# The last layer's experts: each block's down product moved into its own turn

## The reference, cut to what matters

```python
def hier_moe(h, gw, gb, ew, eb, w_gu, w_down):
    ...
    w_sel = jax.nn.softmax(top_v, axis=-1) * p_g
    e_idx = g_sel[:, None] * EXPERTS_PER_GROUP + top_i
    combine = jnp.sum(jax.nn.one_hot(e_idx, N_EXPERTS, dtype=jnp.float32) * w_sel[..., None], axis=1)
    y = jnp.zeros((tok.shape[0], D), jnp.float32)
    for e in range(N_EXPERTS):
        gu = tok @ w_gu[e]
        act = jax.nn.silu(gu[:, :D_EXPERT]) * gu[:, D_EXPERT:]
        y = y + combine[:, e:e + 1] * (act @ w_down[e]).astype(jnp.float32)
    return y.reshape(B, L, D).astype(h.dtype)
```

## Time and profile before

| | |
|---|---|
| time, median of 3 runs | 1123.66 us (1121.16 to 1126.11) |
| profiled execution: its own time | 1126.82 us |
| profiled execution: span | 1125.1 us |
| mean granted TensorE clock over the span | 0.929 |
| from the start of the last layer's first gate_up to the end of its last add_rows | 885.5 to 1114.1 us |
| the same stretch, busy (885 to 1114.2 us) | PE 188.48 us, DVE 56.14 us, ACT 17.03 us, DMA share 0.90 |
| from the last add_rows to the end of the span | 11.0 us |

### The profile page before, as it was taken

The page is one execution under the profiler, slowest core; times in us unless marked ns, Lnnn a source line. Parts: engine busy times, 40 slices in busy tenths (PEclk is TensorE's granted clock), DMA queues, the critical chain, the costliest instruction groups (busy, mean ns, idle before and its releaser), DMA issues.

```text
span 1125.1 us, 24489 instructions
## 1 busy us (share of the span) xinstructions
PE 950.4 (84%) x9652; PEld 595.8 (53%) x9653; DVE 390.4 (35%) x1003; ACT 280.6 (25%) x756; POOL 185.1 (16%) x284
## 2 busy tenths in 40 slices
PE   3999999899999599998996379997998688798785
PEld 2453634555555467666763166664665455455443
DVE  2100026658543512111111184627653622222123
ACT  4122135356433111111110162134644100000001
POOL 0030012310012233433332321014001100000001
PEclk9999999999999599999998679998999698999888
DMA  9983315466233879999999797541314989999991
GB/s 376 366 266 119 150 75 208 183 222 250 75 117 127 347 302 404 422 424 423 423 425 425 255 399 280 225 147 78 114 75 160 383 329 426 425 425 400 429 409 57
DMA packets 54663, 313.53 MB, mean 279 GB/s; under 512 B 12203, under 2 KB 17445, under 8 KB 36021
## 3 DMA queue, kind: packets, MB, share of 16 engines
q1 hardware_dynamic: 33664, 279.19, 61.1%
q0 software_dynamic: 10192, 27.88, 7.0%
q10 hardware_dynamic: 10724, 5.29, 1.6%
HBM read 303.88 MB, written 14.75 MB: 283 GB/s over the span
## 4 chain that ended last, share of the span: by engine, by line
PE 71%; DMA 10%; DVE 7%; issue 5%; ACT 4%; ACTq 2%; POOL 0%; SPq 0%; DVEq 0%; POOLq 0%
PE psum L1005 10%; PE psum L556 8%; PE psum L919 8%; PE psum L786 6%; PE psum L1018 5%; PE psum L584 4%; PE psum L932 3%; DMA R<-in_exp_w_gu_dram 3%; DMA weights<-in_exp_w_gu_dram 3%; PE psum L513 3%; PE psum L680 2%; DMA spare_w<-in_exp_w_down_dram 2%; PE psum L943 2%; PE psum L548 2%; PE psum L795 2%
## 5 line engine op out<-in xcount | busy, mean ns | idle before, releaser
L556 PE MATMUL psum<-hT,weights 128*128 128x512 f32 (+1 forms) x336 | 120.0, 516 | 1.5 <-DVE hT L2110 1.5
L1005 PE MATMUL psum<-weights,lat 128*32 128x256 f32 x1568 | 95.5, 395 | 21.9 <-DMA weights<-in_exp_w_gu_dram 9.7
L919 PE MATMUL psum<-weights,lat 128*32 128x256 f32 x992 | 70.8, 442 | 27.0 <-issue 18.5
L556 PEld LDWEIGHTS psum<-hT,weights 128*128 128x128 f32 x336 | 64.4, 193 | 53.8 <-issue 47.5
L1005 PEld LDWEIGHTS psum<-weights,lat 128*32 128x32 f32 x1568 | 61.4, 114 | 52.3 <-issue 29.6
L1667 DVE TENSOR_REDUCE st<-psum 128x1 f32<-128x512 f32 (+1 forms) x96 | 56.7, 599 | 48.3 <-PE psum L670 20.8
L1824 DVE STREAM_TRANSPOSE lat<-lat 128x256 f32<-128x256 f32 x41 | 18.3, 445 | 151.6 <-PE psum L1005 146.0
L919 PEld LDWEIGHTS psum<-weights,lat 128*32 128x32 f32 x992 | 38.9, 125 | 57.0 <-issue 44.1
L1287 ACT ACTIVATE R<-psum,st 128x512 f32<-128x512 f32 (+1 forms) x78 | 48.0, 616 | 80.1 <-DVE st L1667 48.0
L786 PE MATMUL psum<-weights,hT 128*128 128x512 f32 x144 | 64.9, 606 | 0.0
L1974 DVE TENSOR_TENSOR lat<-lat,psum 128x128 f32<-128x128 f32 x23 | 9.0, 391 | 123.5 <-ACT lat L1431 122.9
(11 more groups left out here) (342 smaller groups left out, 1577.6 us busy)
## 6 DMA issues: line engine op xcount, KB each, us to landing
weights<-in_exp_w_gu_dram SPq DMA_DIRECT2D x42, 2048.0 KB
weights<-in_ada_w_dram SPq DMA_DIRECT2D x24, 2048.0 KB, 8.4
weights<-in_exp_w_down_dram SPq DMA_DIRECT2D x22, 2048.0 KB
hT<-in_exp_w_gu_dram SPq DMA_DIRECT2D x10, 2048.0 KB
R<-in_exp_w_gu_dram SPq DMA_DIRECT2D x10, 2048.0 KB
spare_w<-in_exp_w_down_dram SPq DMA_DIRECT2D x10, 2048.0 KB
weights<-in_w_in_dram SPq DMA_DIRECT2D x6, 2048.0 KB, 15.2
weights<-in_w_out_dram SPq DMA_DIRECT2D x4, 2048.0 KB, 10.1
```

Source lines behind the costliest of these rows:

```text
L556: mm = nc.tensor.matmul(t[:, lo:hi], w[:, k, col:col + P], hT[:, k, lo:hi], start=(k == 0), stop=(k == KD - 1))
L919: mm = nc.tensor.matmul(gu_ps[BLK * j:BLK * j + BLK, 0:256], xgT[:, k, :], w[:, k % 4, j, :, :], start=(k == 0), stop=(k == KD - 1), skip_ ...
L1005: mm = nc.tensor.matmul(gu_ps[BLK * j:BLK * j + BLK, 0:256], xgT[:, k, :], w[:, k % 4, j, :, :], start=(k == 0), stop=(k == KD - 1), skip_ ...
```

## The change

Each block's down product stands in the block's own turn. A turn becomes gate_up(g), select(g + 1), add_rows(g) (which now adds the rows of block g - 1), a wait for the dn piece, down(g). Block 0's turn stands ahead of the loops, with its down product behind the table products. `expert` has one loop body for all of its blocks in place of two. Both tables go into one PSUM bank, and one copy reads them. On ScalarE y_out(g) comes ahead of silu(g); on VectorE rows_turn comes behind the turn of the activations. After the loops only one add_rows is left. The diff:

```diff
             def slot_tables():
-                for job, key, places_ in ((("st", L), ("slot_hot", L), place_token), (("wt", L), ("place_weight", L), place_weight)):
-                    pe.wait_ge(*at(*key))
-                    t = take(*job, banks=(B_TABLE,))
+                t = take("st", L, banks=(B_TABLE,))
+                for which, (key, places_) in enumerate((("slot_hot", place_token), ("place_weight", place_weight))):
+                    pe.wait_ge(*at(key, L))
...
-                def down(done, place):
-                    pe.wait_ge(y_copied, done)
-                    pe.sem_inc(sem("pe_hold"), 1)
-                    pe.wait_ge(actT_ready, done)
+                def down(g, place):
+                    pe.wait_ge(actT_ready, g + 1)
...
-                def block(g, place, place_before, landed=None, in_extra=False):
+                def block(g, place, landed, in_extra=False):
                     gate_up(g, place, landed, in_extra)
                     select(g + 1)
-                    down(g, place_before)
                     add_rows(g)
+                    pe.wait_ge(sem(f"w_dn{place}"), landed[1])
+                    pe.sem_inc(sem("pe_hold"), 1)
+                    down(g, place)
+
+                def expert(triple, place, first=False):
...
+                    if first:
+                        with pe.If(n_blocks > 1):
+                            with pe.Fori(start + 1, start + n_blocks) as g:
+                                block(g, place, both)
+                    else:
+                        with pe.Fori(start, start + n_blocks) as g:
+                            block(g, place, both, in_extra)
...
+                pe.wait_ge(sem("w_dn0"), landed0)
+                down(0, 0)
...
-                    if not first:
-                        block(start, place, (place + 2) % 3, ((L + 1) * 16 if in_extra else landed_lo(L, triple, place), landed), in_extra)
-                    pe.wait_ge(sem(f"w_dn{place}"), landed)
-                    pe.sem_inc(sem("pe_hold"), 1)
-                    with pe.If(n_blocks > 1):
-                        with pe.Fori(start + 1, start + n_blocks) as g:
-                            block(g, place, place, in_extra=in_extra)
...
-                down(total, 0)
                 add_rows(total)
-                add_rows(total + 1)
...
-                act.sem_inc(y_copied, 1)
+                act.sem_inc(sem("rows_added"), 1)
...
                 with act.Fori(1, total) as g:
+                    y_out(g)
                     silu(g)
-                    y_out(g)
...
-                    v.sem_inc(sem("hot_weighted"), 1)
...
-                def weigh_rows(n):
-                    v.wait_ge(sem("rows_added"), n)
+                def weigh_rows(g):
+                    if not isinstance(g, int):
+                        v.wait_ge(sem("rows_added"), g + 1)
...
-                    rows_turn(g + 2)
...
                     nc.vector.transpose(actT[:, :, :].rearrange("p b s -> p (b s)"), act_rows).then_inc(actT_ready, 1)
                     v.wait_ge(actT_ready, g + 1)
+                    rows_turn(g + 2)
                     hot_rows(g + 2)
...
-                v.wait_ge(*at("read", "wt", L))
                 block(0)
+                tables = read(v, "st", L)[:, 0:2 * 64].rearrange("p (w b) -> p b w", w=2)[:, 0:COLS, :]
+                nc.vector.tensor_copy(slot_table[:, :, :], tables).then_inc(*mark("v_route1", ("read", "st", L)))
...
+                weigh_rows(0)
                 with v.Fori(1, total) as g:
                     block(g)
                     weigh_rows(g)
-                weigh_rows(total)
```

More of the change, by code:

```diff
@@ L892, in slot_tables @@
                 L, S = 1, "pe_route1"
-                for job, key, places_ in ((("st", L), ("slot_hot", L), place_token), (("wt", L), ("place_weight", L), place_weight)):
-                    pe.wait_ge(*at(*key))
-                    t = take(*job, banks=(B_TABLE,))
+                t = take("st", L, banks=(B_TABLE,))
+                for which, (key, places_) in enumerate((("slot_hot", place_token), ("place_weight", place_weight))):
+                    pe.wait_ge(*at(key, L))
                     for i in range(4):
                         for a in range(QUADS):
-                            mm = nc.tensor.matmul(t[BLK * a:BLK * a + BLK, 0:COLS], places_[:, i, :], block_last[:, i, :],
+                            mm = nc.tensor.matmul(t[BLK * a:BLK * a + BLK, which * 64:which * 64 + COLS], places_[:, i, :], block_last[:, i, :],
                                                   start=(i == 0), stop=(i == 3), skip_group_check=True)
-                    mm.then_inc(*mark(S, ("filled", *job)))
+                mm.then_inc(*mark(S, ("filled", "st", L)))
             def experts_last():
@@ L945, in add_rows @@
                     mm.then_inc(sem("rows_added"), 1)
-                def block(g, place, place_before, landed=None, in_extra=False):
+                def block(g, place, landed, in_extra=False):
                     gate_up(g, place, landed, in_extra)
                     select(g + 1)
-                    down(g, place_before)
                     add_rows(g)
-                gate_up(0, 0, (landed_lo(L, 0, 0), (uses(0) + 1) * 16))
+                    pe.wait_ge(sem(f"w_dn{place}"), landed[1])
+                    pe.sem_inc(sem("pe_hold"), 1)
+                    down(g, place)
+                def expert(triple, place, first=False):
+                    n_blocks = pe.value_load(tabs[L][0:1, ds(triple * 3 + (T_NB + place), 1)], min_val=1, max_val=MORE + 1)
+                    start = pe.value_load(tabs[L][0:1, ds(triple * 3 + (T_START + place), 1)], min_val=0 if first else 1, max_val=MAXBLK)
+                    landed = (triple + (uses(place) + 1)) * 16
+                    in_extra = isinstance(triple, int) and (triple, place) == (1, 0)
+                    both = ((L + 1) * 16 if in_extra else landed_lo(L, triple, place), landed)
+                    if first:
[5 more added lines that the diff above has]
+                            block(g, place, both, in_extra)
+                landed0 = (uses(0) + 1) * 16
+                gate_up(0, 0, (landed_lo(L, 0, 0), landed0))
                 select(1)
@@ L1939, in route @@
                              rs[:, 9:11, 0:nt].unsqueeze(3).to_broadcast([P, 2, nt, BLK]), ALU.mult), ("place_weight", L))
-                    for which, job in enumerate(("st", "wt")):
-                        nc.vector.tensor_copy(slot_table[:, :, which], read(v, job, L)[:, 0:COLS]).then_inc(*mark(S, ("read", job, L)))
             def rows_turn(count):
@@ L1960, in experts_last @@
                 act_ready, actT_ready, y_done = sem(f"act_ready{L}"), sem(f"actT_ready{L}"), sem(f"y_done{L}")
-                def weigh_rows(n):
-                    v.wait_ge(sem("rows_added"), n)
-                    v.sem_inc(sem("v_hold"), 1)
-                    nc.vector.tensor_copy(slot_now.unsqueeze(1), slot_table[:, ds(n - 1, 1), :]).then_inc(sem("slot_now"), 1)
-                    v.wait_ge(sem("slot_now"), n)
+                def weigh_rows(g):
+                    if not isinstance(g, int):
+                        v.wait_ge(sem("rows_added"), g + 1)
+                        v.sem_inc(sem("v_hold"), 1)
+                    nc.vector.tensor_copy(slot_now.unsqueeze(1), slot_table[:, ds(g, 1), :]).then_inc(sem("slot_now"), 1)
+                    v.wait_ge(sem("slot_now"), g + 1)
                     ts(hot_weight, C("tokens"), slot_now[:, 0:1], slot_now[:, 1:2], ALU.is_equal, ALU.mult).then_inc(sem("hot_weighted"), 1)
@@ L1981, in block @@
                     v.wait_ge(actT_ready, g + 1)
+                    rows_turn(g + 2)
                     hot_rows(g + 2)
                 total = v.value_load(tabs[L][0:1, T_TOTAL:T_TOTAL + 1], min_val=N_EXP, max_val=MAXBLK)
-                v.wait_ge(*at("read", "wt", L))
                 block(0)
+                tables = read(v, "st", L)[:, 0:2 * 64].rearrange("p (w b) -> p b w", w=2)[:, 0:COLS, :]
+                nc.vector.tensor_copy(slot_table[:, :, :], tables).then_inc(*mark("v_route1", ("read", "st", L)))
+                v.wait_ge(*at("read", "st", L))
+                v.wait_ge(*at("banks_zero"))
+                weigh_rows(0)
                 with v.Fori(1, total) as g:
```

## The result

The changed kernel takes 1116.08 us (median of 7 runs, 1111.10 to 1119.89), the kernel before 1123.66 in the same comparison: ratio 0.9921, interval 0.9899 to 0.9944. The forecast was 1112.9 us, ratio 0.9904, with a range of 1109.5 to 1116.5. The first median lies near the upper end of that range, nearer to rival A's 1116.7 than to the forecast, so it is the traces and not this time that tell the two apart. The profiled execution has a span of 1114.4 us; the forecast span was 1114.3.

A forecast was written before the change was run, and what follows sets the result against it. The stage was taken to be bound by a stream of weights that hardly stops. Holes 5.2 + 1.6 and tail 4.0 gave 10.8 us off the median 1123.66: 1112.9 us, range 1109.5 to 1116.5.

The forecast's parts named there:

- rival A: Boundaries between experts keep their length, coming from new code and not from the jump: 1116.7 us, chance 0.10.
- The request and the holes: Earlier dn requests close the weight stream's holes at 904 to 916 and 1012 to 1020 us: 5.2 and 1.6 us gained.
- The start: Block 1's gate_up in the last layer starts at 895.7 us, 0.3 us later than in the kernel before.
- The tail: Behind block 22's gate_up, a down product, an add_rows and a hand-over leave, one add_rows enters: 4.0 us gained.
- The waits in own turn: Down products' waits for dn pieces in their own turn, in the last blocks, don't bite; otherwise 0 to 1 us.
- Rival D: The down product waits in each turn: at 1.5 us a turn the gain is 4.8 us, gone at 1.7; chance 0.05.
- the spare time: TensorE could reach block 19 27 us ahead of its lo piece, 1.5 us a block to spare.
- One body: One loop body shrinks boundaries between experts to 0.81 us; hidden behind the stream, costed at nothing for the end.
- Rival C: Each passage to a loop body, boundary or jump back, costs 3.2 us: 1140.7 us, slower; chance 0.05.
- The reading with two lines: If TensorE keeps only two lines of instructions, a jump back may fetch code again: 1140.7 us.

The follow-up runs named there:

- 150 increments: Changed kernel with two loop bodies again and 150 unused semaphore increments at the start of TensorE's program: 1128.58 us, ratio 1.0023 to the kernel before.
- moved by 130: Kernel before the change with 130 unused semaphore increments at the start of TensorE's program, nothing else: 1132.15 us, ratio 1.0063.

## Why the prediction was right

**The request and the holes.** Forecast: dn at 903.1 and not 909.85, both holes closed, 5.2 + 1.6 us. Measured: 904.82, both closed. The start was worse than forecast: gate_up(1) at 896.62 against 895.7, of which 0.5 is a later start of the stage in this execution, and 1.22 us of idle time inside the table products, unexplained by a wait, was not in the sum. In the changed kernel's second profile that idle time is missing and block 1's gate_up starts 0.7 us nearer to the stage's start; expert 14's hi piece is in use at the same 186 us, so it did not count. Expert 14's hi was in use at 1072.06, in the kernel before at 1078.28: 6.2 us earlier, or 6.7 from the stage's start, against 6.8 forecast. With the request a turn late 5.4 of them were lost again.

**The tail.** Forecast 4.0, measured 13.23 - 8.95 = 4.3 us. The hand-over of y takes 0.45 us between down and add_rows and not 0.74. The stage's gain is then 6.7 + 4.3 + 0.2 = 11.2 us, the 0.2 lying between the hi piece and block 22.

**The waits in own turn.** Forecast 0 to 1 us, with the words that they don't bite; measured 1.02, at block 19, where it counts. The prediction let block 19 ask for dn 5.2 us behind the landing of hi, with 3.3 us for the hi half of gate_up. That half took 3.3 us in the kernel before at half of the clock (granted clock 0.50 from 1076 to 1080 us). In the changed kernel's first profile it ran at the full one (1.00 from 1070 to 1074): select follows 1.7 us behind its start, and TensorE was at the down product before dn had landed. The second profile shows the other case: at a granted clock of 0.50 from 1064 to 1074 us block 19 doesn't wait for dn, but block 20 comes 8.4 us and not 6.6 behind the use of hi. That makes nearly all of the 1.9 us between the two stages. A boundary of 0.83 in place of 1.03 gives some of it back. Rival D doesn't occur: no down product of blocks 1 to 14 waits ahead of L930, and the runs with more work showed the spare time (26 us of the 27 forecast).

**One body.** Costed at nothing for the end, as long as the boundaries shrink to 0.81; they shrank to 0.56 to 0.63 in the written-out part and 0.83 to 1.37 in the loop and behind it. That step held, and with it rival A falls. The price of rival A did not: it put 3.8 us on keeping two bodies, from the idle times of the kernel before. Measured are 7 to 11 us of stage: the idle times themselves grew (ahead of and within the same four gate_ups 14.9 us before, 19.2 with 150 increments), TensorE is granted half of its clock for some microseconds behind each (granted clock 0.50 from 920 to 924 and from 952 to 956 us, 0.57 from 996 to 1000), and the stream then stands nearly still for up to 8 us. That the fuller stream makes the idle times longer is not shown: the kernel before, moved by 130, has 20.0 us of them at the same four. So nearly all of the change's gain needs the one body: own turns without it give nothing (1.0010 and 1.0023). The one body without own turns was not tried.

**Rival C and the lines of code.** A jump back within an expert shows no idle time in any run. The Trainium skill, page "Advanced Engine Details and Errata", section "ISA Cache", gives lines of 256 instructions, "Only 2 cache lines!", and four times the memory on TensorE. By the page's figures of 128KB and 16KB a line that would be eight lines, as an estimate. The runs agree nearly: loops that touch 4 and 7 lines are not fetched again, loops that touch 8 are, at 24 to 36 us. The reading with two lines falls. The prediction asked only whether the loop fits; it did not count where the loop lies. The kernel before stood fewer than ten instructions from the edge of an 8th line, and the change took it away to 4 lines. That the change stayed clear of this edge was luck: with two bodies, where they happened to lie, it would have been 3.1% slower than the kernel before, and no rival had that.

**The size.** Of the 10.8 us the profile shows 10.7 in the span and 11.2 in the stage, the first medians 7.6 and the second 11.4. Runs of the changed kernel differ by 9 and 11 us among themselves in the two comparisons, so this is within what such a comparison can tell. That the forecast span is met to 0.1 us is luck: the stage started 0.5 us later than before, gained 0.4 more than forecast, and executions of one kernel differ by more.

## What to carry to other kernels

A request that waits in one queue for the end of a piece of work should find that work as early in its turn as its inputs allow: on a stream that is otherwise full, each microsecond in which it stood still was about a microsecond of the end here. Count the instructions of a long outer loop: whether it touches 7 or 8 lines of code decided 24 to 36 us here, and an unrelated edit anywhere ahead of it can tip it. A body that is jumped over is not free: behind one TensorE stood idle for 2.5 to 7.7 us here.

## What the runs showed of the hardware

Idle times that end with "issue" ahead of a matmul can be instruction fetches. A fetch is 16 KB. Behind a jump into code that was not fetched yet TensorE stood idle for 2.5 to 7.7 us. The longer of these idle times fell into stretches in which the DMA engines moved 403 to 438 GB/s; the 3.23 us ahead of block 3 before the change fell partly into the stream's hole (86 GB/s from 908 to 912 us). In a loop that touches 8 lines it stood idle for up to 15 us, with three and four fetches in one idle time. Where code runs on from line to line there is next to none: in the changed kernel four lines are fetched between 896 and 921 us, and no gate_up there waits more than 0.63 us. How much of an idle time is due to the full stream was not tried. Why 7 lines fit and 8 don't, if there are eight, stays open; that the line behind the loop is fetched ahead and pushes one out was not tried either.
